# A token transform of Fourier channels folded by sums and differences, and a norm's weight moved into a rounding

## The chip, the cores and the metric

The kernel runs on one core of one Trainium2 chip. The metric is the device time in microseconds of one execution, the median over several runs. The engines are named TensorE (PE), VectorE (DVE), ScalarE (ACT), GpSimd (POOL) and SyncE (SP); they run their own queues in order and meet at semaphores.

## What is computed

Two layers of a hybrid transformer on 512 latent tokens and 256 context tokens, width 1024. After the input projection the columns feed three mixers: windowed attention (8 heads), bidirectional retention (4 heads of 64, with a group norm per head and direction) and a 2-D Fourier mixing of 256 channels in 4 groups. Then an output projection and a squared-ReLU MLP follow. The two parts that the change touches:

```python
def head_group_norm(o, g):
    mu = jnp.mean(o, axis=-1, keepdims=True)
    var = jnp.mean(jnp.square(o - mu), axis=-1, keepdims=True)
    y = (o - mu) * lax.rsqrt(var + EPS)
    return y.reshape(o.shape[0], o.shape[1], -1) * g.astype(jnp.float32)

def fourier_mix(u, w):
    b, l, _ = u.shape
    uf = u.astype(jnp.float32).reshape(b, l, FOURIER_GROUPS, FOURIER_DIM)
    y = jnp.fft.fft2(uf, axes=(1, 3), norm='ortho').real
    return jnp.einsum('blgc,gcd->blgd', y, w.astype(jnp.float32)).reshape(b, l, FOURIER_WIDTH).astype(u.dtype)

def ret_out(o_f, o_b, gf, gb):
    y = (head_group_norm(o_f, gn_g) * jax.nn.silu(gf.astype(jnp.float32))
         + head_group_norm(o_b, gn_g) * jax.nn.silu(gb.astype(jnp.float32)))
    return y.astype(gf.dtype)
```

The last layer computes latent tokens only (the context still gives keys and values).

## The kernel before

Tokens stand in tiles of 128: NL = 4 tiles of latent tokens, and NT = 6 with the context's two. The order of all work is written out by hand, engine by engine; nothing is scheduled. Large products (projections, MLP) are done as three products of rounded parts: a weight `W` and an activation `A` are each split in a high part in the rounded type fp32r and the rest (`Whi`, `Wlo`, `Ahi`, `Alo`). ScalarE rounds, GpSimd subtracts for the weights (L568, L572), VectorE or GpSimd for the activations. The mixers' own products are in fp32.

**The stage of the change** stands in each layer between the input projection and the retention. `Pu` holds the Fourier channels by token, `Pg` the two gates after their silu, `Pr` keys and values of the retention.

- TensorE: turns queries and keys (L1669), multiplies decayed keys with values (`key_values`, L1877, ten steps `e` of four matmuls in two groups: eight ahead of the transform, two within it), transforms the tokens of `Pu` by tables of cosines and sines (L1892: for each of four token tiles, two tables `s` and two halves `c` of the channels; 257 columns; sums in psA for the cosines and psB for the sines). In layer 0 the context follows (L1902, 129 columns, in psS) and, when ScalarE and VectorE have copied all of it out, the channel transform of the context (L1913). Then the retention starts in `psA` (L1936), `psS` (L1958, L1944).
- VectorE: centres the values (`centre`, L1381, L1382), then makes the running states `SD` out of the key-value products in PSUM (`states`, L1415: ten steps of four small instructions, each step after the one two before it), then copies the sine half out of psB, the second half mirrored with its sign turned (L1424, L1426). Then it serves the retention (L1456, L1442, L1467, L1468, L1472).
- ScalarE: rounds half of the keys (`key_hi`, L917) when the third token tile is done, copies psA out (L923, L924), in layer 0 the context (L929, L930), then the other half of the keys.
- GpSimd: decays the keys (L654, ten products of two SBUF tensors), the queries of the first two tiles (L662, four), multiplies the gates `Pg` with the group norm's weight `gng` (L670, one for each token tile, which VectorE's L1467 waits for by `gg_ready`), clears `klk` (L676) and subtracts the rounded keys (L683).
- SyncE: loads the tables, a token tile at a time, in two buffers of `modraw` and one of its own, `dft3`. The weight `gng` is loaded to all partitions by `tmp_load` (L407).

In the retention the normed, gated sum of both directions is turned by TensorE into channels by tokens (L1669) and rounded into `Ahi` (L964, ScalarE, both 128-channel halves in one instruction) and `Alo` (L1472, VectorE).

`rows` and `parT` hold the small parameters: rows of 128 loaded at the start (L414 to L419), turned once by TensorE, so that each becomes a column of `parT`.

## Time and profile before

| | us |
|---|---|
| median of three runs | 1614.09 |
| the runs | 1612.60, 1614.09, 1614.53 |
| the profiled execution | 1613.24 |
| its span in the profile | 1611.3 |

The profile is of one execution. The span runs from the first to the last instruction; 1.9 us of the execution's time lie around it. Start times are counted from the span's start. Lengths of single TensorE instructions overlap, since matmuls are pipelined: how long one holds the engine is read from start to start. The same holds, by some 0.1 us, for ScalarE and VectorE.

### The profile page before, as it was taken

Reading aid. Unit: us, or ns where it says so; the run is one execution under the profiler, and the core shown is the slowest. Engines: PE = TensorE matmul, PEld = TensorE weight load, DVE = VectorE, ACT = ScalarE, POOL = GpSimd, SP = SyncE. Lnnn points to the kernel's source line nnn. Section 1 sums busy time; section 2 is a strip of 40 time slices with the busy share of each in tenths; the row PEclk is TensorE's granted clock in tenths of the full one; section 3 lists DMA queues with packets and bytes.
Section 4 is the critical chain, followed back from the end, with each engine's and each line's share of the span. In section 5 each row is a group of like instructions: output and inputs, shape, how many; then the busy total and the mean of one; then the engine's idle time right before and its main releaser. Section 6 shows DMA issues by size and latency. Waiting matters only on the chain.

```text
span 1611.3 us, 22758 instructions
## 1 busy us (share of the span) xinstructions
PE 1566.2 (97%) x8730; PEld 1343.1 (83%) x8730; DVE 916.9 (57%) x1440; ACT 590.0 (37%) x958; POOL 651.2 (40%) x355
## 2 busy tenths in 40 slices
PE   6899999999999999999999999999999999999999
PEld 2688888988888888888888888888897788888887
DVE  5778977766765656445454668696644433333322
ACT  4532246752532221222212244434753522323222
POOL 1426678922333322232232453337004444444442
PEclk9899999999999999999999999999999999999999
DMA  9344203024233444354343533222002233333333
GB/s 330 98 131 129 75 27 109 26 66 131 85 105 118 131 122 131 89 156 131 110 128 103 153 98 103 66 88 71 17 1 79 78 93 93 103 91 101 94 97 100
DMA packets 170616, 163.43 MB, mean 101 GB/s; under 512 B 6672, under 2 KB 134176, under 8 KB 170528
## 3 DMA queue, kind: packets, MB, share of 16 engines
q1 hardware_dynamic: 170528, 162.20, 33.0%
q8 instruction: 63, 1.03, 0.3%
q14 instruction: 25, 0.20, 0.0%
HBM read 160.08 MB, written 2.10 MB: 101 GB/s over the span
## 4 chain that ended last, share of the span: by engine, by line
PE 90%; DVE 3%; issue 2%; ACT 2%; DMA 2%; POOL 1%; SPq 0%; POOLq 0%; ACTq 0%
PE psA L2043 10%; PE psB L2043 10%; PE psA L2044 10%; PE psA L2045 10%; PE psB L2044 10%; PE psB L2045 10%; PE ps L2018 4%; PE psS L1669 2%; PE psA L1827 2%; PE psA L1828 2%; PE psA L1829 2%; PE psB L1827 2%; PE psB L1828 2%; PE psB L1829 2%; PE ps L1669 1%
## 5 line engine op out<-in xcount | busy, mean ns | idle before, releaser
L568 POOL TENSOR_TENSOR Wlo<-raw,Whi 128x1024 fp32r<-128x1024 f32 x156 | 379.9, 2436 | 787.2 <-ACT Whi L734 787.2
L734 ACT ACTIVATE Whi<-raw 128x1024 fp32r<-128x1024 f32 x181 | 191.7, 1060 | 695.9 <-PE psB L2045 350.9
L2043 PE MATMUL psB<-Ahi,Whi 128*128 128x512 f32 (+1 forms) x432 | 154.5, 358 | 1.8 <-POOL Wlo L714 1.1
L2043 PE MATMUL psA<-Ahi,Whi 128*128 128x512 f32 (+1 forms) x424 | 152.1, 359 | 3.4 <-POOL Wlo L568 1.7
L2044 PE MATMUL psB<-Alo,Whi 128*128 128x512 f32 (+1 forms) x432 | 153.8, 356 | 0.0
L2045 PE MATMUL psB<-Ahi,Wlo 128*128 128x512 f32 (+1 forms) x432 | 153.7, 356 | 0.0
L2044 PE MATMUL psA<-Alo,Whi 128*128 128x512 f32 (+1 forms) x424 | 150.7, 355 | 0.0
L2045 PE MATMUL psA<-Ahi,Wlo 128*128 128x512 f32 (+1 forms) x424 | 150.7, 355 | 0.0
L1310 DVE SCALAR_TENSOR_TENSOR X<-psB,modT,X 128x256 f32<-128x256 f32 (+1 forms) x104 | 67.2, 665 | 130.5 <-PE psB L2045 130.4
L2043 PE MATMUL psA<-Hhi,Whi 128*128 128x512 f32 (+1 forms) x368 | 131.8, 358 | 3.1 <-DVE X L1310 2.9
L2043 PE MATMUL psB<-Hhi,Whi 128*128 128x512 f32 (+1 forms) x368 | 131.6, 358 | 0.1
L2044 PE MATMUL psB<-Hlo,Whi 128*128 128x512 f32 (+1 forms) x368 | 131.3, 357 | 0.0
L2045 PE MATMUL psB<-Hhi,Wlo 128*128 128x512 f32 (+1 forms) x368 | 131.1, 356 | 0.0
L2044 PE MATMUL psA<-Hlo,Whi 128*128 128x512 f32 (+1 forms) x368 | 130.8, 356 | 0.0
L2045 PE MATMUL psA<-Hhi,Wlo 128*128 128x512 f32 (+1 forms) x368 | 130.8, 355 | 0.0
L1310 DVE SCALAR_TENSOR_TENSOR X<-psA,modT,X 128x256 f32<-128x256 f32 (+1 forms) x104 | 67.0, 663 | 92.3 <-PE psA L2045 92.2
L1140 DVE SCALAR_TENSOR_TENSOR macc<-modraw,csil,macc 128x512 f32<-128x512 f32 x126 | 113.7, 959 | 9.8 <-DMA modraw<-in_w_mod_dram 9.8
L1535 DVE TENSOR_TENSOR Hlo<-Ab,Hhi 128x512 fp32r<-128x512 f32 (+2 forms) x68 | 72.7, 1070 | 54.5 <-ACT Hhi L1016 54.5
L1533 DVE TENSOR_TENSOR Ab<-psA,Tb 128x512 f32<-128x512 f32 (+2 forms) x34 | 26.7, 785 | 129.4 <-ACT Tb L1008 129.4
L2043 PEld LDWEIGHTS psA<-Ahi,Whi 128*128 128x128 f32 x424 | 80.1, 189 | 16.3 <-POOL Wlo L568 2.4
L2043 PEld LDWEIGHTS psB<-Ahi,Whi 128*128 128x128 f32 x432 | 81.7, 189 | 14.0 <-POOL Wlo L714 1.5
L2045 PEld LDWEIGHTS psB<-Ahi,Wlo 128*128 128x128 f32 x432 | 81.6, 189 | 11.7
(352 smaller groups left out, 3575.1 us busy)
## 6 DMA issues: line engine op xcount, KB each, us to landing
raw<-in_w_ff_dram SPq DMA_DIRECT2D x135, 512.0 KB, 4.1
modraw<-in_w_mod_dram SPq DMA_DIRECT2D x72, 512.0 KB, 4.3
raw<-in_w_in_dram SPq DMA_DIRECT2D x36, 512.0 KB, 3.8
modst<-in_w_mod_dram SPq DMA_DIRECT2D x16, 512.0 KB, 5.9
raw<-in_w_out_dram SPq DMA_DIRECT2D x16, 512.0 KB, 3.7
modat<-in_w_mod_dram SPq DMA_DIRECT2D x8, 512.0 KB, 4.2
macc<-in_w_ff_dram SPq DMA_DIRECT2D x5, 512.0 KB, 3.7
Xin<-in_x_dram SPq DMA_DIRECT2D x8, 256.0 KB, 8.1
```

The costliest lines, as they stand in the source:

```text
L568: nc.gpsimd.tensor_tensor(Wlo[:, s, :], raw[:, s, :], Whi[:, s, :], ALU.subtract).then_inc(S["lo_done"], 1)
L734: nc.scalar.activation(whis[slot], raws[slot], ACT.Copy).then_inc(S["hi_done"], 1)
L1140: ins = V.scalar_tensor_tensor(out=acc[:, s, :], in0=src[:, kk * MCH:(kk + 1) * MCH], scalar=col, in1=acc[:, s, :], op0=ALU.mult, op1=ALU.add)
L1310: last = V.scalar_tensor_tensor(out=X[:, m, c0:c1], in0=pair[p][:, c0:c1], scalar=modT[:, l, 8 * chunk + m, s:s + 1], in1=X[:, m, c0:c1], ...
L1535: V.tensor_tensor(Hlo[:, hpar, k, c0:c1], Ab[:, k % 2, c0:c1], Hhi[:, hpar, k, c0:c1], ALU.subtract).then_inc(S["h_lo"], 1)
L1827: mm(out, ah, wh, start=first, stop=False)
L1828: mm(out, ah, wl, start=False, stop=False)
L1829: last = mm(out, al, wh, start=False, stop=fin)
L2018: last = mm((ps6, ps7)[b % 2][:, h * HD:(h + 1) * HD], PTs[:, it % 2, i * P:(i + 1) * P], Pk[:, kt, P + (h // 4) * HD:P + (h // 4 + 1) * H ...
L2043: mm(dst[:, c0:c1], wh, hi_[:, i, c0:c1], start=first, stop=False)
L2044: mm(dst[:, c0:c1], wh, lo_[:, i, c0:c1], start=False, stop=False)
L2045: last = mm(dst[:, c0:c1], wl, hi_[:, i, c0:c1], start=False, stop=fin)
```

## The change

The transform of the tokens uses that a discrete Fourier transform over 512 tokens, split by four, needs only products over 128 tokens. With x0 to x3 the four token tiles of `Pu`, VectorE makes x0+x2, x1+x3, x0-x2, x1-x3, and from the first two their sum and difference (`folds`, six instructions of 128x256, all from SBUF to SBUF; in layer 0 two more for the context, x4+x5 and x4-x5). They stand in VectorE's queue between the centring and the states. TensorE multiplies the sum with a table for the frequencies 0, 4, 8, ..., the difference with one for 2, 6, 10, ..., and x0-x2 and x1-x3 with two for the odd ones. Each product holds a cosine part and a sine part, and writes every fourth or every second column of psA, half a bank for the channels' first half and half for the second. psB is no longer used for it. The context is split by two in the same manner. The table for a layer is one load of 128x768 (before: four of 128x514), for the context 128x256.

Since cosines and sines now stand in the same bank, ScalarE copies one half of the channels out and VectorE the other, in four instructions each instead of two. Two columns that are always zero are cleared by GpSimd.

The group norm's weight is no longer multiplied into the gates on GpSimd (L670 goes, and so does its broadcast load). It is loaded as four rows beside the other small parameters, turned with them, and applied as a scale for each partition where the turned result is rounded: L964 becomes two instructions of ScalarE, one for each half, and L1472 two of VectorE.

TensorE in layer 0, from the key-value products to the retention, before (`modraw` and `dft` are the tables, `ret_scratch` the decayed keys):

```order
L1877 MATMUL ps<-Pr,ret_scratch 128x128 x8
L1877 MATMUL psS<-Pr,ret_scratch 128x128 x8
L1892 MATMUL psA<-modraw,Pu 128x257 x2
L1892 MATMUL psB<-modraw,Pu 128x257 x2
L1892 MATMUL psA<-modraw,Pu 128x257 x2
L1892 MATMUL psB<-modraw,Pu 128x257 x2
L1892 MATMUL psA<-dft,Pu 128x257 x2
L1892 MATMUL psB<-dft,Pu 128x257 x2
L1877 MATMUL ps<-Pr,ret_scratch 128x128 x4
L1892 MATMUL psA<-modraw,Pu 128x257 x2
L1892 MATMUL psB<-modraw,Pu 128x257 x2
L1902 MATMUL psS<-modraw,Pu 128x129 x8
```

and after (here `ret_scratch` holds the folds as well):

```order
L1894 MATMUL ps<-Pr,ret_scratch 128x128 x8
L1894 MATMUL psS<-Pr,ret_scratch 128x128 x8
L1910 MATMUL psA<-modraw,ret_scratch 128x128 x4
L1894 MATMUL ps<-Pr,ret_scratch 128x128 x4
L1910 MATMUL psA<-modraw,ret_scratch 128x256 x4
L1919 MATMUL psS<-modraw,ret_scratch 128x128 x4
```

The last key-value step moved from behind three quarters of the transform to behind its first, short half.

VectorE in layer 0, from the last centring on, before:

```order
L1382 SCALAR_TENSOR_TENSOR Pr<-vm,Pr 128x256
L1415 SCALAR_TENSOR_TENSOR SD<-SD,CD,ps 64x64 x16
L1415 SCALAR_TENSOR_TENSOR SD<-SD,CD,psS 64x64 x16
L1415 SCALAR_TENSOR_TENSOR SD<-SD,CD,ps 64x64 x8
L1424 COPY ret_scratch<-psB 128x2x257
L1426 TENSOR_SCALAR ret_scratch<-psB 128x2x255
```

and after:

```order
L1378 SCALAR_TENSOR_TENSOR Pr<-vm,Pr 128x256
L1420 TENSOR_TENSOR ret_scratch<-Pu 128x256
L1421 TENSOR_TENSOR ret_scratch<-Pu 128x256
L1422 TENSOR_TENSOR ret_scratch<-Pu 128x256
L1423 TENSOR_TENSOR ret_scratch<-Pu 128x256
L1425 TENSOR_TENSOR ret_scratch<-ret_scratch 128x256
L1426 TENSOR_TENSOR ret_scratch<-ret_scratch 128x256
L1429 TENSOR_TENSOR ret_scratch<-Pu 128x256
L1430 TENSOR_TENSOR ret_scratch<-Pu 128x256
L1411 SCALAR_TENSOR_TENSOR SD<-SD,CD,ps 64x64 x16
```

Eight instructions now stand ahead of the states; in layer 1 it is six. The diff, cut to its core:

```diff
@@ SyncE
-            sp.dma_start(gng[:, :], a["ret_gn_g"][l].partition_broadcast(P)).then_inc(S["tmp_in"], 16)
+        sp.dma_start(rows[48:52, 1, :], a["ret_gn_g"].rearrange("l (t p) -> (l t) p", p=P)).then_inc(con, 16)
-            for k in range(2):
-                m_load(w + k, (w + k) % 2, dft_home(l, k)[:, 0:2 * FL], a["dft_lat"][k])
-            if l:
-                sp.wait_ge(S["mod_used"], DFT_FIRST[0] + 3 - MOD0)
-            sp.dma_start(dft3[:, :], a["dft_lat"][2]).then_inc(S["dft_in"], 16)
...
+            m_load(w, w % 2, dft_home(w, LAT_W), a["dft_lat"])
+            if l == 0:
+                m_load(w + 1, (w + 1) % 2, dft_home(w + 1, CTX_W), a["dft_ctx"])
@@ GpSimd
-            for t in range(TT[l]):
-                pool.wait_ge(S["p_ready"], evac_index[l, 3, t])
-                nc.gpsimd.tensor_tensor(Pg[:, t, :].rearrange("p (d n) -> p d n", d=2), Pg[:, t, :].rearrange("p (d n) -> p d n", d=2),
-                                        gng[:, :].unsqueeze(1).to_broadcast([P, 2, 256]), ALU.mult).then_inc(S["gg_ready"], 1)
+            nc.gpsimd.memset(zs_at(1)[:, :, 0:FL:FL - 1], 0.0).then_inc(S["zs_zero"], 1)
@@ ScalarE
-            za = psA[:, :].rearrange("p (a b) -> p a b", a=2)
-            nc.scalar.activation(zs_at(0)[:, :, 0:FL], za[:, :, 0:FL], ACT.Copy)
-            nc.scalar.activation(zs_at(0)[:, :, FL:LAT], za[:, :, LAT - FL:0:-1], ACT.Copy).then_inc(S["za_evac"], 1)
+            za = psA[:, 0:512]
+            nc.scalar.activation(zs_at(0)[:, 0, 0:FL], za[:, 0:FL], ACT.Copy)
+            nc.scalar.activation(zs_at(0)[:, 0, FL:LAT], za[:, LAT - FL:0:-1], ACT.Copy)
+            nc.scalar.activation(zs_at(1)[:, 0, 1:FL - 1], za[:, FL:LAT], ACT.Copy)
+            nc.scalar.activation(zs_at(1)[:, 0, FL:LAT], za[:, LAT - 1:FL - 1:-1], ACT.Copy, scale=-1.0).then_inc(S["za_evac"], 1)
...
+                    for q in range(2):
+                        last = nc.scalar.activation(Ahi[:, 4 + q, t * P:(t + 1) * P], (ps6, ps7)[t % 2][:, q * P:(q + 1) * P], ACT.Copy, scale=parT[:, 48 + 2 * l + q:49 + 2 * l + q])
@@ VectorE
+            def folds():
+
+                dve.wait_ge(S["unit_done"], UP * (l + 1))
+                dve.wait_ge(S["p_ready"], evac_index[l, 4, NL - 1])
+                x = [Pu[:, t, :] for t in range(NT)]
+                V.tensor_tensor(fold_half(0), x[0], x[2], ALU.add).then_inc(S["fold_half"], 1)
+                V.tensor_tensor(fold_half(1), x[1], x[3], ALU.add).then_inc(S["fold_half"], 1)
+                V.tensor_tensor(fold(2), x[0], x[2], ALU.subtract).then_inc(S["fold_ready"], 1)
+                V.tensor_tensor(fold(3), x[1], x[3], ALU.subtract).then_inc(S["fold_ready"], 1)
+                dve.wait_ge(S["fold_half"], 2 * l + 2)
+                V.tensor_tensor(fold(0), fold_half(0), fold_half(1), ALU.add).then_inc(S["fold_ready"], 1)
+                V.tensor_tensor(fold(1), fold_half(0), fold_half(1), ALU.subtract).then_inc(S["fold_ready"], 1)
+                if l == 0:
+                    dve.wait_ge(S["p_ready"], evac_index[0, 4, NT - 1])
+                    V.tensor_tensor(fold(4), x[4], x[5], ALU.add).then_inc(S["fold_ready"], 1)
+                    V.tensor_tensor(fold(5), x[4], x[5], ALU.subtract).then_inc(S["fold_ready"], 1)
+
+            folds()
             dve.wait_ge(S["sd_zero"], 1)
             dve.wait_ge(S["prep_act"], 15 * (l + 1))
             states(0, NST_E)
@@ TensorE
+            pe.wait_ge(S["fold_ready"], (0, 6)[l] + 4)
+            lat_tab = dft_home(w, LAT_W)
+            for k, (first, step, t0, n) in enumerate(((0, 4, 0, P), (2, 4, P, P), (1, 2, 2 * P, 2 * P), (1, 2, 4 * P, 2 * P))):
+                if k == 2:
                     key_values(8, NST_E)
...
+                for c in range(2):
+                    last = mm(psA[:, c * 512 + first:c * 512 + 512:step], fold(k)[:, c * P:(c + 1) * P], lat_tab[:, t0:t0 + n], start=(k < 3), stop=(k != 2))
```

## Rows read from the trace of the kernel before

**Rows 1.** The page's first part: busy time of TensorE over the whole span

```profile
PE 1566.2 (97%) x8730; PEld 1343.1 (83%) x8730; DVE 916.9 (57%) x1440; ACT 590.0 (37%) x958; POOL 651.2 (40%) x355
```

**Rows 2.** Timeline, TensorE, layer 0: start us, length, line, tiles, count [idle, releaser]

```profile
214.88 1.03 PE L1892 MATMUL psA<-modraw,Pu 128*128 128x257 f32 x4
...
220.09 1.05 PE L1877 MATMUL ps<-Pr,ret_scratch 128*128 128x128 f32 x8
...
222.72 1.95 PE L1902 MATMUL psS<-modraw,Pu 128*128 128x129 f32 x16
...
226.06 1.97 PE L1913 MATMUL psB<-Zc,WCS 128*128 128x256 f32 x8 [1.39 <-ACT Zc L930]
```

**Rows 3.** Timeline, VectorE, layer 0

```profile
209.86 0.43 DVE L1382 SCALAR_TENSOR_TENSOR Pr<-vm,Pr 128x256 f32<-128x256 f32 x1
210.20 0.41 DVE L1381 TENSOR_REDUCE vm<-Pr 128x4 f32<-128x256 f32 x1
210.65 0.43 DVE L1382 SCALAR_TENSOR_TENSOR Pr<-vm,Pr 128x256 f32<-128x256 f32 x1
212.51 4.05 DVE L1415 SCALAR_TENSOR_TENSOR SD<-SD,CD,ps 64x64 f32<-64x64 f32 x16 [1.44 <-PE ps L1877]
...
221.25 2.01 DVE L1415 SCALAR_TENSOR_TENSOR SD<-SD,CD,ps 64x64 f32<-64x64 f32 x8 [0.61 <-PE ps L1877]
...
223.30 0.69 DVE L1424 COPY ret_scratch<-psB 128x514 f32<-128x514 f32 x1
```

**Rows 4.** Timeline, GpSimd, layer 0: three L654 singly, then the four L662

```profile
209.93 0.83 POOL L654 TENSOR_TENSOR ret_scratch<-Pr,ZE 128x256 f32<-128x256 f32 x1
...
210.72 0.83 POOL L654 TENSOR_TENSOR ret_scratch<-Pr,ZE 128x256 f32<-128x256 f32 x1
...
211.51 0.61 POOL L654 TENSOR_TENSOR ret_scratch<-Pr,ZE 128x256 f32<-128x256 f32 x1
...
214.94 2.78 POOL L662 TENSOR_TENSOR ret_scratch<-rqT,XQ 128x256 f32<-128x256 f32 x4
```

**Rows 5.** Timeline, VectorE, layer 0, earlier: instructions queued beside GpSimd's

```profile
146.15 4.91 DVE L1140 SCALAR_TENSOR_TENSOR macc<-modraw,csil,macc 128x512 f32<-128x512 f32 x3
```

**Rows 6.** Timelines, TensorE and then VectorE, layer 1

```profile
1108.74 1.03 PE L1892 MATMUL psB<-modraw,Pu 128*128 128x257 f32 x4
...
1111.57 0.72 PE L1936 MATMUL psA<-rqT,rkT 64*128 64x128 f32 x8 [1.80 <-ACT ret_scratch L924]
...
1121.17 2.00 PE L1944 MATMUL psS<-Pr,ret_scratch 128*128 128x64 f32 x16
...
1123.30 1.16 PE L1958 MATMUL psS<-SD,ret_scratch 128*128 128x128 f32 x8
...
1099.14 4.05 DVE L1415 SCALAR_TENSOR_TENSOR SD<-SD,CD,ps 64x64 f32<-64x64 f32 x16 [11.10 <-PE ps L1877]
...
1108.14 2.01 DVE L1415 SCALAR_TENSOR_TENSOR SD<-SD,CD,ps 64x64 f32<-64x64 f32 x8 [0.87 <-PE ps L1877]
...
1113.64 2.08 DVE L1442 TENSOR_TENSOR qs<-qT,qs 64x512 fp32r<-64x512 f32 x1
```

**Rows 7.** Four stretches: length, PE busy (count), the others; PEclk, DMA share, GB/s

```profile
942.80:946.20 3.40, 3.40 (x28) 3.28 (x27) 1.48 (x2) 0.63 (x1) 0.18 (x1) 1.00 0.50 154
...
949.90:953.30 3.40, 3.40 (x19) 3.40 (x18) 0.48 (x1) 1.70 (x3) 2.98 (x2) 0.50 0.00 0
...
965.90:968.70 2.80, 0.00 (x0) 0.00 (x0) 2.80 (x4) 0.77 (x2) 1.78 (x1) 1.00 0.68 187
...
45.50:55.60 10.10, 7.52 (x20) 5.54 (x21) 9.72 (x17) 5.74 (x12) 1.81 (x1) 0.50 0.20 60
```

**Rows 8.** Timeline, SyncE's queue, start of the kernel

```profile
2.99 0.28 SPq L419 DMA_DIRECT2D rows<-in_c_ctx_dram  x1
```

**Rows 9.** Groups by form, ScalarE: busy, mean ns of one | idle before

```profile
L811 ACT ACTIVATE decay<-tmpt,lgt 128x128 f32<-128x128 f32 x16 | 5.1, 389 | 0.0
...
L964 ACT ACTIVATE Ahi<-ps 128x256 fp32r<-128x256 f32 x10 | 3.7, 373 | 0.6 <-PE ps L1669 0.6
```

More of the change, by code:

```diff
@@ L24 @@
 FL, FC = LAT // 2 + 1, CTX // 2 + 1
+LAT_W, CTX_W = 6 * P, 2 * P
 GROUPS = [(0, 512), (512, 512), (1024, 512), (1536, 512), (2048, 256)]
@@ L256, in mod_loads, with dft_home, fold, fold_half @@
     def mod_loads(w):
-        return (w - MOD0) // 2 + 1 - ((4 if w % 2 else 5) if w >= LATE else 0)
-    def dft_home(l, k):
-        return dft3[:, :] if k == 2 else modraw[:, (DFT_FIRST[l] + k % 3) % 2, :]
-    def dft_wait(engine, l, k):
-        w = DFT_FIRST[l] + k % 3
-        if k == 2:
-            engine.wait_ge(S["dft_in"], 16 * (l + 1))
-        else:
-            engine.wait_ge(mod_in[w % 2], 16 * (mod_loads(w) + k // 3))
+        return (w - MOD0) // 2 + 1 - ((5 if w % 2 else 6) if w >= LATE else 0)
+    def dft_home(w, n):
+        return modraw[:, w % 2, 0:n]
+    def fold(i):
+        return rs[:, 18 + i // 2, (i % 2) * 256:(i % 2) * 256 + 256]
+    def fold_half(i):
+        return rs[:, 6 + i, 0:256]
     def thirds(x):
@@ L1471, in retention @@
                     dve.wait_ge(S["rT_hi"], r + 1)
-                    V.tensor_tensor(Alo[:, 4:6, t * P:(t + 1) * P], (ps6, ps7)[t % 2][:, 0:256].rearrange("p (a b) -> p a b", a=2),
-                                    Ahi[:, 4:6, t * P:(t + 1) * P], ALU.subtract).then_inc(S["rT_lo"], 1)
+                    for q in range(2):
+                        last = V.scalar_tensor_tensor(out=Alo[:, 4 + q, t * P:(t + 1) * P], in0=(ps6, ps7)[t % 2][:, q * P:(q + 1) * P], scalar=parT[:, 48 + 2 * l + q:49 + 2 * l + q],
+                                                      in1=Ahi[:, 4 + q, t * P:(t + 1) * P], op0=ALU.mult, op1=ALU.subtract)
+                    last.then_inc(S["rT_lo"], 1)
                 if 1 <= s < TT[l] + 1:
@@ L2285, in dft @@
         return (np.stack([np.cos(w), np.sin(w)]) / np.sqrt(n * HD)).astype(f)
-    lat = dft(LAT).reshape(2, NL, P, FL).transpose(1, 2, 0, 3).reshape(NL, P, 2 * FL)
-    ctx = dft(CTX).reshape(2, 2, P, FC).transpose(2, 0, 1, 3).reshape(P, 4 * FC)
+    (lc, ls), (xc, xs) = [[part[0:P] for part in dft(n)] for n in (LAT, CTX)]
+    odd = np.arange(1, LAT // 2, 2)
+    turn = np.where(odd % 4 == 1, f(1), f(-1))
+    lat = np.concatenate([lc[:, 0::4], ls[:, 4:FL - 1:4], lc[:, 2::4], ls[:, 2::4], lc[:, odd], ls[:, odd],
+                          -turn * ls[:, odd], turn * lc[:, odd]], 1).astype(f)
+    ctx = np.concatenate([xc[:, 0::2], xs[:, 2:FC - 1:2], xc[:, 1::2], xs[:, 1::2]], 1).astype(f)
     return {"table": tab, "dft_lat": np.ascontiguousarray(lat), "dft_ctx": np.ascontiguousarray(ctx)}
```

74 lines of the change are left out of this document (34 added, 40 removed).

## The prediction

> **What bounds the kernel now.** I read the page first: TensorE is busy for 97% of the span [rows 1], so a microsecond counts where TensorE waits, or where its own work shrinks while nothing else is late. The change touches one place in each of the two layers, so I then read the order of time there, engine by engine. In layer 0 TensorE runs the token transform from 214.88 (L1892), one step of the key-value products in its middle (L1877 at 220.09), then the context's transform (L1902 at 222.72), and stops until 226.06 [rows 2]. The reader should see the other queue beside it: VectorE turns the key-value products into states (L1415) from 212.51, eight of the forty from 221.25, and only then copies psB out, from 223.30 [rows 3]. TensorE's row at 226.06 names ScalarE's last copy of the context (L930) as what it waited 1.39 us for [rows 2]. So at the end of this stage two chains arrive close together: VectorE's (states, two copies of 0.6) at about 224.6 and ScalarE's at 225.9. In layer 1, with no context, it is TensorE's last products at 1108.74, VectorE's last states at 1108.14 and the two copies after them, TensorE again at 1111.57 [rows 6]; that row names ScalarE's copy, but by its length VectorE's second copy ended last, 0.1 us before. TensorE's matmuls here are therefore not alone on the path: the forty states take as long as they do.
>
> **Matmuls removed.** A 128x257 product is two instructions; four take 0.87 us (214.88, 1.03 is the end of the last), so 0.43 a product; a 128x128 one 0.22 (eight instructions to 220.98, where 0.89 have passed) [rows 2]. Sixteen of 257 columns (6.9 us) become four of 128 and four of 256 (0.9 + 1.7 = 2.6): 4.3 us less in each layer; eight context products of 129 columns (1.8) become four of 128 (0.9). The new products write every second or fourth column of psA. No row shows that; if it cost double it would still be inside the waits found below, so it is zero on the path and at worst 1 us.
>
> **Layer 0, the queue of VectorE.** The eight sums and differences (`folds`) stand between the centring and the states. Centring ends at 211.05 (last step 210.65 + 0.43; the next instruction can start 0.34 after such a one, as at 209.86 and 210.20) and the first state starts at 212.51 [rows 3]: 1.46 us are free. At their own pace, 0.34 each, the folds need 2.7 and push the states by 1.3. But GpSimd runs ten products of two SBUF operands (L654) until 214.94 and four more (L662) after it [rows 4], and each fold too reads two tensors from SBUF. What that does the rows show. Beside the centring steps one L654 takes 0.83 us, alone 0.61, and beside VectorE they start 0.785 apart [rows 4]: GpSimd loses about 0.2 each time, less than one centring step. When VectorE has such instructions queued without a gap it is VectorE that is slow: three L1140 of 512 elements, beside a long and a short GpSimd product, take 4.91 us, 1.6 each [rows 5]. So the two take turns, one instruction each. Folds back to back against L654 then go at 0.785 each: the first reads after the product that started at 210.72, and ends at 211.85; the sixth at 215.8, the eighth, against L662, at 217.4. The states start at 217.4 instead of 212.51.
>
> From there the sum runs on: TensorE may start the transform at 215.9 (it needs the sixth fold), does the two short pairs until 216.8, and waits for the first eight states until 219.5 before L1877's last step (0.9) and the long pairs (1.7): 222.1. The context waits for 32 states, 217.4 + 8.2 = 225.6, ends at 226.6, and ScalarE's four copies of it end at 227.7. The forty states, now without the 0.6 us in which VectorE waited for TensorE, end at 217.4 + 10.24 = 227.7. The copy out is now four instructions of 255 or 257 columns at 0.34 = 1.4, for two that took 1.2 [rows 3]. TensorE goes on at 229.1, after 226.06: **+3.1**. What is late next is VectorE; the shorter matmuls lie wholly in its shadow. The lower bound for this term is folds at their own pace: states at 213.8, copies done at 225.5, TensorE at 225.7: -0.4.
>
> The Trainium skill ("SBUF — State Buffer", section "Who interferes with whom") says that a VectorE instruction with two SBUF inputs contends with a GpSimd one that reads SBUF, and that the later one blocks for the whole of the other's. By it a fold waits for a full product, and eight cost 8 x (0.34 + 0.61) = 7.6 us instead of 6.3: TensorE 1.3 us later still. The trace agrees with the rule in kind (0.83 us against 0.61 [rows 4]), not in size, and its own 0.785 is what I use.
>
> **Layer 1.** VectorE sits idle for 11 us before the states, until 1099.14 [rows 6], and all of Pu was copied out before TensorE began the turns, some 6 us earlier, so the six folds are hidden whichever pace they have; if that cover were gone they would cost 2 to 4.7 us. TensorE ends its transform at 1105.4 instead of 1109.7. VectorE's states lose the 0.87 us that they waited for L1877 [rows 6] and end at 1109.3; four copies, 1.4; TensorE starts at 1110.8 instead of 1111.57: -0.8. The gain norm product L670 is gone from GpSimd, so the subtraction of the keys (L683) runs before 1111 and no longer beside VectorE's L1442, which took 2.08 us in a first go of two. TensorE, otherwise without a pause from 1111.57, was late by 0.2 at 1121.17 and by 0.3 at 1123.30, where sixteen L1944 need 1.8 [rows 6]: -0.5 more, at least 0. **-1.25** for the layer.
>
> **Rounding with the weight.** One L964 of 256 columns, 0.37 us, becomes two of 128 with a scale from a tensor; such an instruction (L811) takes 0.39 [rows 9] and can start some 0.3 after the one before it. In the last two steps this stands between TensorE's turn and the softmax's table load, 0.3 each: +0.45 a layer, **+0.9**; between 0 (if hidden) and 1.5. On VectorE one instruction becomes two, 0.1 us each time, hidden by the turn to the next step. Dropping L670 from GpSimd is worth nothing beyond the above: L1467 was never late for it.
>
> **The start.** One more DMA (four rows) stands in SyncE's queue ahead of the first weights. The one before it takes 0.28 us and starts at 2.99 [rows 8], and what follows is the stream of loads that the start of the kernel waits for. **+0.35**, at least 0 and at most 0.5. The two broadcasts of the weight (L407) and three table loads a layer less are off the path: their destinations are long filled.
>
> **The clock.** TensorE would stand still in layer 0 from 216.8 to 219.5, 222.1 to 225.6 and 226.6 to 229.1, in layer 1 from 1105.4 to 1110.8. In this trace an idle stretch of 2.8 us (965.9) left the granted clock at 1.00, 2.4 GHz; but it was 0.50, 1.2 GHz, in 45.5 to 55.6, after a stretch with 2.8 us of no work and gaps inside, and for 3.4 us at 949.9, after TensorE had summed squares with matmuls of one column for 2.6 us [rows 7]. 3.5 and 5.4 us are longer than what it held through. So I expect one fall in each layer. At 1.2 GHz 19 instructions start in 3.4 us for 28 [rows 7], 1.1 us lost; over 4 to 5 us, as after 51, 1.5 us. Take 1.45 twice: **+2.9**, between 0 and about 6.
>
> **Sum.** 3.1 - 1.25 + 0.9 + 0.35 + 2.9 = 6.0. The profiled execution took 1613.24 (span 1611.3): 1619.2. That is 0.85 below the median of the runs, 1614.09, so against the median the sum would be 1620; I keep the sum as it is, since one execution lies as well at one end of the runs as at the other.
>
> **Rivals.**
> A, forecast: turns at the port and a fall of the clock in each layer: 1619.2, own range 1616.8 to 1621.5. Chance 0.45.
> B: the turns, but the clock holds: 1616.3. For it: it held through 2.8 us. Chance 0.18, within 0.2% of 1614.09 (3.2 us).
> C, the other side (not slower): VectorE gets its eight folds in at 0.34 while GpSimd waits, as the centring steps did, which were not slowed themselves (0.43) [rows 3]; the whole rests on whether VectorE's queue without gaps keeps the port. It decides from the point at which the folds end before 214. Then layer 0 gives -0.4, the sum -0.4 - 1.25 + 0.9 + 0.35 = -0.4, 1612.8, and with one or two falls of the clock up to 1615.7. Against it: the 1.6 us of [rows 5]. Chance 0.18.
> D, faster: the transform's matmuls are the path after all, as they would be if the states' chain kept step with them; 4.3 + 0.9 in layer 0 and 4.3 in layer 1 are saved but for the folds' 1.3: some 8 us less, 1605. Against it: VectorE's chain ends at 224.6, 1.3 us ahead of TensorE's restart, whatever TensorE does. Chance 0.07.
> E: the clock stays at 1.2 GHz through much of the retention stage, whose matmuls are short (64 and 128 columns); each 3.4 us more costs 1.1 to 1.7. 1623 to 1628. Chance 0.12.
>
> A measurement of this kernel can tell about 0.2%, 3.2 us, from no change. Slower by more than that: most of A (0.4), E and the top of B, 0.57; within: 0.34; faster: D and a little of C, 0.09. The range leaves out D and the upper part of E: 1612.5 to 1623.5; A and B and C lie in it.
>
> **What would show it.** The time from the last centring step to the first state in layer 0: 6.3 us (A, B) or 2.7 (C); one fold at 0.75 to 0.8 us or at 0.42. GpSimd's ten L654 in 7.7 us. TensorE's restart: 229.5 in layer 0 with the start's 0.35, and, in layer 1, 1110.8 plus what came before. The granted clock below 1.00 in both places. The rounding's two activations at 0.39. I am wrong if TensorE restarts in layer 0 before 226, if the strided products themselves take several times 0.43, or if the stretch after retention is slower for another reason than these.

## The result, and the profile after

| | before | changed |
| --- | --- | --- |
| median of five runs each, us | 1613.62 | 1619.91 |
| ratio to before, 95% interval | | 1.0044, 1.0033 to 1.0055 |
| the profiled execution, us | 1613.24 | 1619.91 |
| its span, us | 1611.3 | 1617.9 |
| mean granted clock of TensorE | 0.996 | 0.991 |

The kernel became slower: by 6.3 us from median to median, and by 0.44%, which is 7.1 us, by the ratio, an estimate over all executions that need not be the quotient of the medians (1.0039). Run once more beside the experiments its ratio was 1.0054 (1.0035 to 1.0073). Medians and ratios here are of fast executions alone; beside them one of the changed kernel took 2232.67 us, at a mean granted clock of 0.65, and one of before 3156.01. The forecast was 1619.2.

The timelines of layer 0, VectorE first: start, length, engine, line, tiles, and in brackets the idle time before and what ended it. They answer to [rows 3].

```profile
210.47 0.43 DVE L1378 SCALAR_TENSOR_TENSOR Pr<-vm,Pr 128x256 f32<-128x256 f32 x1
210.81 0.83 DVE L1420 TENSOR_TENSOR ret_scratch<-Pu 128x256 f32<-128x256 f32 x1
211.57 0.83 DVE L1421 TENSOR_TENSOR ret_scratch<-Pu 128x256 f32<-128x256 f32 x1
...
216.09 0.94 DVE L1430 TENSOR_TENSOR ret_scratch<-Pu 128x256 f32<-128x256 f32 x1
216.96 4.04 DVE L1411 SCALAR_TENSOR_TENSOR SD<-SD,CD,ps 64x64 f32<-64x64 f32 x16
...
225.11 2.01 DVE L1411 SCALAR_TENSOR_TENSOR SD<-SD,CD,ps 64x64 f32<-64x64 f32 x8
227.15 0.43 DVE L1438 COPY ret_scratch<-psA 128x257 f32<-128x257 f32 x1
...
228.15 0.41 DVE L1441 TENSOR_SCALAR ret_scratch<-psA 128x255 f32<-128x255 f32 x1
```

Each fold takes 0.83 and starts 0.755 after the one before. The states begin at 216.96 instead of 212.51, and behind them stand the four copies: there is no idle time left in VectorE's queue. GpSimd beside it [rows 4]:

```profile
208.21 7.67 POOL L647 TENSOR_TENSOR ret_scratch<-Pr,ZE 128x256 f32<-128x256 f32 x10
```

And TensorE [rows 2]:

```profile
215.56 1.13 PE L1910 MATMUL psA<-modraw,ret_scratch 128*128 128x128 f32 x8 [0.41 <-DVE ret_scratch L1426]
219.10 2.05 PE L1894 MATMUL ps<-Pr,ret_scratch 128*128 128x128 f32 x8 [2.41 <-DVE SD L1411]
220.94 2.61 PE L1910 MATMUL psA<-modraw,ret_scratch 128*128 128x256 f32 x8
225.22 1.13 PE L1919 MATMUL psS<-modraw,ret_scratch 128*128 128x128 f32 x8 [1.67 <-DVE SD L1411]
228.67 3.22 PE L1930 MATMUL psB<-Zc,WCS 128*128 128x256 f32 x8 [2.31 <-DVE ret_scratch L1441]
231.82 1.09 PE L1953 MATMUL psA<-rqT,rkT 64*128 64x128 f32 x8
```

All four waits of TensorE are now ended by VectorE. It restarts at 228.67 (the first product after the last wait of the stage), before at 226.06. Layer 1, VectorE and then TensorE [rows 6]:

```profile
1100.11 2.59 DVE L1423 TENSOR_TENSOR ret_scratch<-Pu 128x256 f32<-128x256 f32 x1
...
1104.90 4.05 DVE L1411 SCALAR_TENSOR_TENSOR SD<-SD,CD,ps 64x64 f32<-64x64 f32 x16 [0.69 <-PE ps L1894]
...
1116.11 0.41 DVE L1441 TENSOR_SCALAR ret_scratch<-psA 128x255 f32<-128x255 f32 x1
```

```profile
1109.93 1.89 PE L1910 MATMUL psA<-modraw,ret_scratch 128*128 128x256 f32 x8
1116.63 1.21 PE L1953 MATMUL psA<-rqT,rkT 64*128 64x128 f32 x8 [4.81 <-DVE ret_scratch L1441]
1117.77 2.07 PE L1975 MATMUL psS<-SD,ret_scratch 128*128 128x128 f32 x8
```

The transform is out of TensorE's way by 1111.8, and TensorE waits 4.81 us for the states and the copies. That the new products write every second column of psA costs nothing that shows: eight instructions of 128x256 take 1.89 (1109.93), where L1913, of the same size, took 1.97 [rows 2].

Last, the stretches in which the granted clock was 0.50, which is 1.2 GHz (from:to, length, TensorE busy and its instructions, clock, DMA share, GB/s); they answer to [rows 7]. Between 25 us and the last two of the span, the trace of before has two such stretches: 10.2 us from 45.4, and 3.4 us from 949.9.

```profile
44.90:55.14 10.24, 7.19 (x20) 0.50 0.20 61
218.98:222.39 3.41, 3.29 (x12) 0.50 0.01 2
229.22:232.63 3.41, 3.41 (x15) 0.50 0.03 5
403.30:406.71 3.41, 3.41 (x18) 0.50 0.76 251
973.33:976.74 3.41, 3.41 (x18) 0.50 0.45 148
1116.69:1120.10 3.41, 3.41 (x18) 0.50 0.00 0
```

One more, of 3.4 us, is at 952.9, where before had its own at 949.9. The fall at 973.33 comes 0.3 us behind a wait of TensorE that the kernel before has too, the 2.8 us from 965.9 of [rows 7], after which the clock held:

```profile
973.05 0.36 PE L2060 MATMUL psA<-Hhi,Whi 128*128 128x256 f32 x1 [2.87 <-DVE X L1306]
```

**Where the 6.6 us of the span came in.** The same TensorE instruction was looked up in both traces, and the start of before taken from the start of after:

| TensorE's instruction | late by, us | step |
| --- | --- | --- |
| first turn after the projection, 204.79 | -0.30 | -0.30 |
| restart in layer 0, 228.67 | 2.61 | +2.91 |
| first L1961 of retention, 234.57 (fall at 229.2) | 3.93 | +1.32 |
| after the rounding's last tile, 271.36 | 4.02 | +0.09 |
| 437 (fall at 403.3) | 5.55 | +1.53 |
| 464.25, after a wait in the feed-forward | 4.57 | -0.98 |
| 923 to 973 (one fall in each trace) | 4.29 | -0.28 |
| 978 to 1099 (fall at 973.3) | 5.76 | +1.47 |
| restart in layer 1, 1116.63 | 5.06 | -0.70 |
| 1119.77 (fall at 1116.7) | 6.47 | +1.41 |
| 1129.43 | 6.13 | -0.34 |
| 1138.33, after the rounding's last tile | 6.51 | +0.38 |

### The profile page after: what moved, and what is told of

Same layout as the page of the kernel before. It is cut to its first block, busy times and chain, and to the rows that moved or that the text cites. A ratio compares the mean times of both kernels' runs of the same rounds, so it can differ in the third digit from the quotient of the medians.

```text
span 1617.9 us, 22707 instructions
## 1 busy us (share of the span) xinstructions
PE 1566.8 (97%) x8690; PEld 1341.9 (83%) x8690; DVE 924.0 (57%) x1468; ACT 592.7 (37%) x972; POOL 642.7 (40%) x349
## 4 chain that ended last, share of the span: by engine, by line
PE 91%; DVE 3%; ACT 2%; DMA 2%; issue 1%; POOL 1%; SPq 0%; ACTq 0%; DVEq 0%; POOLq 0%
PE psA L2060 10%; PE psB L2060 10%; PE psB L2061 10%; PE psA L2061 10%; PE psA L2062 10%; PE psB L2062 10%; PE ps L2035 4%; PE psS L1686 2%; PE psA L1844 2%; PE psA L1845 2%; PE psA L1846 2%; PE psB L1844 2%; PE psB L1846 2%; PE psB L1845 2%; PE ps L1686 1%; PE psS L1846 1%
## 5 line engine op out<-in xcount | busy, mean ns | idle before, releaser
L561 POOL TENSOR_TENSOR Wlo<-raw,Whi 128x1024 fp32r<-128x1024 f32 x156 | 381.8, 2448 | 784.0 <-ACT Whi L725 784.0
```

Of the source, the lines that this page charges most:

```text
L561: nc.gpsimd.tensor_tensor(Wlo[:, s, :], raw[:, s, :], Whi[:, s, :], ALU.subtract).then_inc(S["lo_done"], 1)
```

## Experiments

In each, the executions of the kernel before on the same chip are the measure (medians 1614.9, 1613.86, 1613.8 and 1614.42 in four groups). Behind a time stand, in brackets, its ratio to them and the ratio's 95% interval. "Net" of a shift means: after what TensorE was already late by at the first turn, or ahead of the stage, is taken off.

### The two halves of the change, each alone

`fold_alone` is the changed kernel with group norm's weight back on GpSimd; `weight_alone` is the kernel before with the weight in the rounding. The second one's core:

```
-  nc.scalar.activation(Ahi[:, 4:6, t * P:(t + 1) * P], (ps6, ps7)[t % 2][:, 0:256].rearrange("p (a b) -> p a b", a=2), ACT.Copy).then_inc(S["rT_hi"], 1)
+  for q in range(2):
+      last = nc.scalar.activation(Ahi[:, 4 + q, t * P:(t + 1) * P], (ps6, ps7)[t % 2][:, q * P:(q + 1) * P], ACT.Copy, scale=parT[:, 48 + 2 * l + q:49 + 2 * l + q])
+  last.then_inc(S["rT_hi"], 1)
```

> The changed kernel with group norm's weight put back where it was (product L670 on GpSimd, one rounding instruction per tile, broadcasts of the weight, no extra DMA at the start); the transform stays split by four. Theory: the 6.3 us of the change are the transform's: VectorE's queue in layer 0 (+2.9 at the restart), the granted clock after the waits (+1.3 to +1.5 a layer), -0.7 in layer 1, and the rounding adds 0.8 to 1.0. Then this kernel is 5.0 to 5.5 us slower than before, 1618.6 to 1619.1. Rival: the rounding and its weight are the larger part, since in both layers the stretch after the restart is the one that grows (3.9 to 4.4 in layer 0, 6.1 to 6.5 in layer 1): then it is 2 to 4 us above before, 1615.5 to 1617.5.

> The kernel before with the weight moved into the rounding alone (no L670, two activations and two VectorE instructions per tile, one more DMA at the start, three loads less); transform as before. Theory: +0.4 to +0.5 a layer at the last tile, where two activations stand between the turn and the softmax's table load, less 0.3 at the start: +0.5 to +0.9, 1614.1 to 1614.5. Layer 1's L1442 at 0.7 instead of 2.1 us and its restart otherwise as before. Rival: the weight is what costs, +2.5 to +4 (1616 to 1617.5).

Measured: `fold_alone` 1621.54 (ratio 1.0048, 1.0030 to 1.0066), `weight_alone` 1614.98 (1.0003, 0.9994 to 1.0011). The whole loss belongs to the transform; the weight costs nothing that can be told. `fold_alone` is 6.6 us above its group's before by the medians and 7.7 by the ratio (4.8 to 10.7), more than the 5.0 to 5.5 expected; one of its six executions took 1629.34. That the longer stretch after the restart was the rounding's, the rival, is out. On ScalarE the expected thing does happen. The last tile in layer 1, of before and then of `weight_alone`:

```profile
1129.29 0.39 ACT L964 ACTIVATE Ahi<-ps 128x256 fp32r<-128x256 f32 x1 [0.32 <-PE ps L1669]
1129.69 1.28 ACT L981 ACT_TABLE_LOAD   x1
```

```profile
1129.96 0.63 ACT L957 ACTIVATE Ahi<-ps,parT 128x128 fp32r<-128x128 f32 x2 [0.26 <-PE ps L1665]
1130.61 1.28 ACT L975 ACT_TABLE_LOAD   x1
```

From the turn's end to the table load 0.65 instead of 0.40. TensorE is later by 0.43 at 256 us, but 0.41 of it is given back at 268 us, where it waits for the softmax of a later item anyway; in layer 1 it is -0.48 by 1123.8 (GpSimd is free of L670) and +0.38 by 1132.7. VectorE's L1442 of before took 1.48 here, not the 0.7 expected: GpSimd's second subtraction of keys waits for ScalarE's rounding of them, starts at 1113.78 and still stands beside it.

### Folds later in the queue

`late4`, from the changed kernel, layer 0 only:

```
-  folds()
...
-  states(0, NST_E)
+  states(0, 4)
+  folds()
+  states(4, NST_E)
```

> The changed kernel; in layer 0 VectorE does the first 16 of the 40 states before its eight sums and differences, so that GpSimd's products have mostly ended when they come. Theory (turns at the port): the states start at 212.2 and the folds at 216.3, two of them at 0.78 and six at 0.34, 3.6 us instead of 6.3; the states end at 226.0, TensorE restarts at 227.5 instead of 228.67: 1.0 to 1.3 us less, 1618.7, and GpSimd's ten products end by 214.9. Rival: it is not GpSimd that makes the folds 0.755 apart but the folds themselves (a first pass over these tiles, a fixed cost in layer 0): they stay at 0.75, 6.0 us, and the restart stays at 228.4 to 228.7, 1619.9.

Measured: 1618.39 (1.0031, 1.0016 to 1.0046). VectorE in layer 0:

```profile
217.85 0.71 DVE L1420 TENSOR_TENSOR ret_scratch<-Pu 128x256 f32<-128x256 f32 x1
218.48 0.94 DVE L1421 TENSOR_TENSOR ret_scratch<-Pu 128x256 f32<-128x256 f32 x1
219.34 0.41 DVE L1422 TENSOR_TENSOR ret_scratch<-Pu 128x256 f32<-128x256 f32 x1
219.68 0.41 DVE L1423 TENSOR_TENSOR ret_scratch<-Pu 128x256 f32<-128x256 f32 x1
```

The first two, beside GpSimd's L655, take 0.71 and 0.94; from 219.1 on GpSimd only zeroes, and the other six go at 0.34. Eight folds in 3.6 us instead of 6.2, as the theory said; that the folds are slow by themselves is out. TensorE's restart gains less than the 1.0 to 1.3 expected, 0.65 net of the start's shift, since the transform now begins only at 220.91 and ScalarE's copies of the context come last there.

### What a turn is made of

`half_folds` lets the folds of layer 0 work on 128 of 256 columns (first line added, `c` being those columns; the transform takes the same 128 for both halves of the channels, so the second half's transform is left out and the result is not the kernel's), `stt_folds` writes them in the form of the centring steps (second line added):

```
-  V.tensor_tensor(fold(2), x[0], x[2], ALU.subtract).then_inc(S["fold_ready"], 1)
+  V.tensor_tensor(fold(2)[:, c], x[0], x[2], ALU.subtract).then_inc(S["fold_ready"], 1)
...
+  V.scalar_tensor_tensor(out=fold(2), in0=x[0], scalar=1.0, in1=x[2], op0=ALU.mult, op1=ALU.subtract).then_inc(S["fold_ready"], 1)
```

> The changed kernel; in layer 0 the eight sums and differences take 128 of their 256 columns, and the transform takes the same 128 for both halves (so the second half's transform is left out). Is the 0.755 us between folds the sum of both engines' work (0.34 and about 0.4), or one GpSimd product with VectorE's inside it? Theory (turns, where the wait for GpSimd's product sets the pace): a fold loses 0.14 us of its own work, the spacing falls to 0.6 to 0.66. Rival (a fold is taken up only at GpSimd's next boundary, and GpSimd's product of 0.61 plus a fixed cost is the period): the spacing stays at 0.74 to 0.76.

> The changed kernel with the sums and differences written as SCALAR_TENSOR_TENSOR (operand times 1.0, then plus or minus the other) as the centring steps are. Theory: the turns come from two tensors read from SBUF, whatever the form: 0.75 apart, as before, 1619.9. Rival: the form TENSOR_TENSOR alone takes turns, since centring's L1378 beside L647 takes 0.43: then the folds go at 0.34 to 0.45, the states start 2.5 to 3 us earlier, 1617.

Each ran once, for its trace (1617.56 and 1620.12 us). Measured, `half_folds` and then `stt_folds`:

```profile
212.03 0.70 DVE L1423 TENSOR_TENSOR ret_scratch<-Pu 128x128 f32<-128x128 f32 x1
212.65 0.70 DVE L1424 TENSOR_TENSOR ret_scratch<-Pu 128x128 f32<-128x128 f32 x1
```

```profile
211.91 0.83 DVE L1421 SCALAR_TENSOR_TENSOR ret_scratch<-Pu 128x256 f32<-128x256 f32 x1
212.67 0.83 DVE L1422 SCALAR_TENSOR_TENSOR ret_scratch<-Pu 128x256 f32<-128x256 f32 x1
```

Half the columns shorten the period, from the start of one fold to the next, from 0.755 to 0.62, by 0.135. That is the difference between undisturbed instructions of VectorE with two tensors from SBUF (0.41 with 256 columns in `late4`, 0.29 with 128, L1359 at 203.70 in the changed kernel), so the fold's own work counts in full. The rest, 0.755 less the 0.336 between undisturbed folds, is 0.42. The simplest reading is that it is the part of GpSimd's product during which a fold can't read; a product takes 0.61 alone [rows 4], and undisturbed ones start 0.57 apart (ten L654 in 5.76, 1096.56 in before). The form makes no difference. Why the centring steps of the same form were spared beside GpSimd's short products is not shown; in them every second instruction, the reduction, reads one tensor only. Beside a long product they were not spared: one L1382 took 2.29 at 206.42 in before, with L568 of 2.37 started at 206.06. The Trainium skill ("SBUF — State Buffer", "Who interferes with whom") says that a VectorE instruction with two SBUF inputs contends with a GpSimd one that reads SBUF, and these runs agree. The section calls the ports that the two share an exclusive lock. If that held for the whole of each instruction, a period would be a fold and a whole product, 0.34 and 0.57 to 0.61, so 0.91 to 0.95; 0.755 is what was measured.

### The clock

`clock_held` gives TensorE something to do in the waits of the change: matmuls whose result nobody reads, called idle matmuls from here on. The calls of `hold` stand in layer 0 before L1894's last step (two matmuls), before the context (one) and before the restart (two), in layer 1 before the restart (five):

```
+  def hold(bank, n):
+      for i in range(n):
+          mm(bank, fold(0)[:, 0:P], lat_tab[:, 0:512], start=True, stop=True)
...
+  hold(psB[:, 0:512], (2, 5)[l])
   pe.wait_ge(S["za_evac"], l + 1)
```

> The changed kernel with matmuls of 512 columns into psB, whose result nobody reads, in TensorE's waits: two and one and two in layer 0 (before L1894's last step, before the context, before the restart), five in layer 1 before the restart. Theory: 2.5 to 4 us of the change's 6.3 are the granted clock, which falls to 1.2 GHz at 219.0, 229.2 and 1116.7: with TensorE kept at work it stays at 1.00 there, TensorE is 1.3 less late by 255 us and 1.4 less in layer 1: 2.7 less, 1617.2, and the executions lie closer together than those of the changed kernel. Rival: the matmuls stand in the way of the restart themselves, or the clock falls all the same: 1619.5 to 1621.

Measured: 1618.15 (1.0022, 1.0013 to 1.0030), where the changed kernel has 1.0044 and 1.0054: 3.5 us less by the first, with some 2 either way. By the medians it is 4.3 above before instead of 6.3, 2.0 less. Stretches of its trace:

```profile
226.27:229.68 3.41, 3.41 (x11) 0.51 0.00 0
1112.00:1117.00 5.00, 4.50 (x11) 1.00 0.01 2
1117.00:1120.40 3.40, 3.40 (x33) 1.00 0.03 5
```

In layer 1 the clock stays at 2.4 GHz, and 33 instructions start in 3.4 us after the restart, where the changed kernel had 18. In layer 0 one fall of two is left; at 1.2 GHz the last two idle matmuls took 2.8 us and pushed the restart by 0.7. In the two traces, net of the start, the held kernel gains 0.7 behind layer 0's restart and 1.6 in layer 1. So the clock in these waits is a third to half of the loss, and the runs don't tell more exactly.

### Where the copies stand

`scalar_copies`: ScalarE copies psA's upper half, four instructions of which one is shown; VectorE ends with the states.

```
-  V.tensor_copy(zs_at(0)[:, 1, 0:FL], zb[:, 0:FL])
+  nc.scalar.activation(zs_at(0)[:, 1, 0:FL], zb[:, 0:FL], ACT.Copy)
```

> The changed kernel with the second half of the transform (psA's upper 512 columns) copied out by ScalarE instead of VectorE, four more activations in its queue. Theory: VectorE's chain (folds, states, copies) sets the restart in both layers, so taking the 1.4 us of copies from its end brings the restart to 227.7 in layer 0 (ScalarE's copies of the context are then last) and to 1115.3 plus the shift of layer 0 in layer 1: 1.0 and 1.3 less, in all 1.5 to 2.3 us less, 1617.6 to 1618.4. Rival: ScalarE's queue is as late as VectorE's, and its four more copies of 0.3 put the context's copies behind: restart 228.6 in layer 0, only layer 1's 1.2 gained, 1618.7 to 1619.

Measured: 1627.34 (1.0071, 1.0052 to 1.0089), 1618.6 to 1629.3. The waits behave as the theory said: net of the shift before them, the restart in layer 0 is 0.9 sooner than in the changed kernel (228.39, ScalarE last), in layer 1 it is 1.5 sooner. And yet the kernel is slower, for this:

```profile
1109.60:1112.90 3.30, 0.04 (x1) 1.00 0.00 0
1114.54:1135.02 20.48, 20.48 (x103) 0.50 0.24 68
```

The clock, after a wait of 3.3 us, fell and stayed at 1.2 GHz for 20.5 us of retention, all of it in TensorE's way: TensorE is 1.4 late at the restart and 10.6 late by 1139 us. That is rival E of the prediction. A wait of 3.3 instead of 4.8 us did not save the clock. Nor does the wait alone decide: one execution of the six took 1618.6, at a mean granted clock of 0.990 where the others have 0.982 to 0.986. The changed kernel has such an execution too, one in ten: 1629.25 in `changed_again`, at 0.984, where its other nine lie from 1619.6 to 1622.9 at 0.987 to 0.992. `fold_alone` and `late4` have one each (1629.34, 1628.74, both 0.984).

### Do the falls at 403 and 973 belong to the change?

`delayed_before2` is the kernel before with 4.35 us of idle matmuls ahead of layer 0's L1913:

```
+  for i in range(5):
+      mm(psB[:, 0:512], WCS[:, 0, 0, :], zs_at(0)[:, 0], start=True, stop=True)
```

> The kernel before with nothing of the change, but five matmuls of 512 columns (into psB, read by nobody) after layer 0's waits and ahead of the context's second transform: TensorE at work for 4.35 us more, everything after it later by that, and no idle stretch added. What it asks: do the falls of the clock that the changed kernel shows at 403 and 973, after one-column matmuls that the kernel before has too, come with a later start of the stage alone? Theory (they have nothing to do with the change's waits; which of the stages falls is a matter of when it comes): such falls appear here too, and the time is 4.35 to 6.5 us above before, the excess over 4.35 being up to 2.2. Rival (they are the consequence of the change's idle stretches or of its falls at 219 and 229): the clock stays at 1.00 at about 400 and falls only at about 950 as in before, and the time is 4.2 to 4.6 above before.

Measured: 1619.23 (1.0029, 1.0020 to 1.0039), 4.7 above before.

```profile
403.43:406.84 3.41, 3.41 (x19) 0.51 0.69 236
950.70:954.10 3.40, 3.40 (x33) 1.00 0.17 56
973.43:976.84 3.41, 3.25 (x15) 0.50 0.49 154
```

Both falls are there without anything of the change, and the one that before has at 949.9 is not. What TensorE does ahead of the three places is the same in every kernel: one-column matmuls that sum squares ahead of the first two, a wait of 2.9 us ahead of the third. That the falls come with a later start fits, but is not the whole of it. At about 400 the clock falls with TensorE 4.45 late there (`stt_folds`) and not with 4.56 or 4.59 (`late4`, `half_folds`); it falls in `gpsimd_folds_held2`, where TensorE is less than 0.4 us from its place in before. What decides is not shown. Over ten executions the extra falls are worth about 0.4 us beyond the 4.35 that were put in (by the ratio, from -1.1 to +1.9), less than the 2.2 that this one profile shows (TensorE 4.02 later than before at 230, 6.25 at 977), and their mean granted clock, 0.993 to 0.995, is that of before's (0.993 to 0.996). So in the difference of two profiles such a fall is luck; in the medians little of it is left.

### A version without the queue

`gpsimd_folds_held`, `gpsimd_folds` and `gpsimd_folds_held2` take the folds of layer 0 off VectorE, and the copies too, as in `scalar_copies`. The latent folds (`G` is GpSimd's tensor_tensor) stand between its last two weight splits, with the half sums `m` in macc and the results in parts of modraw that the tables leave free; the context's two stand behind the decayed queries. In `gpsimd_folds_held2` TensorE has two idle matmuls before it waits for the context's folds, one before layer 0's restart, three before layer 1's.

```
+  low_part(18)
+  G(m[0], x[0], x[2], ALU.add).then_inc(S["fold_half"], 1)
+  G(m[1], x[1], x[3], ALU.add).then_inc(S["fold_half"], 1)
+  G(fold0(2), x[0], x[2], ALU.subtract).then_inc(S["fold_ready"], 1)
...
+  low_part(19)
...
   decayed_queries(1)
+  nc.gpsimd.tensor_tensor(fold(4), Pu[:, 4, :], Pu[:, 5, :], ALU.add).then_inc(S["fold_ctx"], 1)
```

> A version meant to keep what the change saves. From the changed kernel: group norm's weight back as before; in layer 0 the six latent sums and differences run on GpSimd at 201 to 205 us, before its last weight split (L561), into free parts of modraw, with halves in macc, and the context's two on GpSimd after the first decayed queries; VectorE goes from centring to the states; ScalarE copies psA's upper half too; matmuls that nobody reads hold the clock in the waits (three and one in layer 0, five in layer 1). Theory: states in layer 0 at 212.3, ended at 222.6, TensorE restarts at 223 instead of 226.06 of the kernel before (-2.9), and in layer 1 1.9 sooner (states' end sets it, no copies behind them): -4.8 in all, 1609 to 1610. Rival: GpSimd's six products take turns with VectorE's L1359 and L1363 at 200 to 204, which TensorE's turns wait for, and what is won in the stages goes there: within 2 us of before, 1612 to 1615.

Measured: 1617.61 (1.0018, 1.0009 to 1.0026), a miss. In this version the weight was back on GpSimd, and the zeroing that TensorE's restart waits for stood behind it:

```profile
222.17 7.38 POOL L687 TENSOR_TENSOR Pg<-Pg,gng 128x512 f32<-128x512 f32 x6
229.49 0.11 POOL L689 MEMSET ret_scratch<- 128x4 f32 x1
229.53 0.11 POOL L691 MEMSET Zc<- 128x4 f32 x1
```

TensorE restarted at 229.85; the states had ended at 225.25 and ScalarE's copies at 227.3. With the weight in the rounding, as the change has it, those products are gone:

> From the changed kernel, with its rounding (group norm's weight stays in it): in layer 0 the six latent sums and differences on GpSimd at 203 us, the context's two on GpSimd behind the decayed queries, GpSimd's zeroing right behind them; ScalarE copies psA's upper half as well. Nothing holds the clock. Theory: in the version with the weight restored, TensorE's restart of layer 0 at 229.85 waited for GpSimd's zeroing at 229.5, behind six products L687 of 7.4 us; without them the zeroing is at 222.5 and the states' end sets the restart: 225.5 with a start late by 1.3, so 1.8 sooner than before; 1.9 sooner in layer 1; rounding +0.9. Before the clock that is -2.8; the clock falls in one or both layers, +1.3 to +9 (as in the version with ScalarE's copies, where it lasted 20 us): 1612.5 to 1620, and executions that lie far apart. Rival: the restart stays later than 227, for another wait: above 1616 even with the clock held.

> The same with matmuls that nobody reads in TensorE's waits, fewer than in the first version and each ended before the work that follows: two before the wait for the context's sums, one before layer 0's restart, three before layer 1's. Theory: -2.8 as above and the clock held in layer 1 and mostly in layer 0: 1611 to 1613, 1 to 3 us below before. Rival: the falls of the clock in layer 0 come whatever is put there (with such matmuls it fell at 226.3 once), +1.3, and the rounding's stage is longer than its two instructions: 1613.5 to 1615.5.

> The changed kernel once more, on the chip and beside the runs of before that the two versions below share. Theory: its time is one sum with a part that varies, the falls of the clock, of which the trace has three more than before's in 218 to 230 and 1117 and two single ones at 403 and 973: 1618 to 1622, ratio 1.003 to 1.0055. Rival (the first result was one chip's): within 0.2% of before.

Measured on one chip: `changed_again` 1620.62 (1.0054, 1.0035 to 1.0073); `gpsimd_folds` 1624.24 (1.0052, 1.0035 to 1.0069), its twelve executions in two groups, four from 1614.6 to 1615.6 and eight from 1623.8 to 1627.5; `gpsimd_folds_held2` **1612.67 (0.9988, 0.9979 to 0.9997)**, all executions from 1610.2 to 1614.7 (before on that chip: 1611.4 to 1617.3). TensorE of the last:

```profile
223.03 1.13 PE L1950 MATMUL psS<-modraw,ret_scratch 128*128 128x128 f32 x8 [0.51 <-DVE SD L1441]
...
225.55 1.97 PE L1962 MATMUL psB<-Zc,WCS 128*128 128x256 f32 x8 [0.53 <-ACT Zc L954]
...
1112.10 0.72 PE L1985 MATMUL psA<-rqT,rkT 64*128 64x128 f32 x8 [0.75 <-issue]
```

The restart comes 0.9 before that of the kernel before in layer 0 (net of a start late by 0.35) and 2.2 before it in layer 1, and the clock is 1.00 behind both. In layer 0 half of what was expected is missing: GpSimd's six folds (202.67 to 208.17) stand beside VectorE's work ahead of the centring, where two products of 128 columns take 0.70 and 0.71 instead of 0.29. The centring begins at 206.70 instead of 204.39, and TensorE waits for it:

```profile
213.48 2.02 PE L1915 MATMUL ps<-Pr,ret_scratch 128*128 128x128 f32 x16 [1.66 <-DVE Pr L1408]
```

The same kernel without the six idle matmuls lies 11 to 15 us above that version's median in eight of twelve executions. That this is the clock, the granted clock of each execution shows: 0.989 to 0.990 in the four short ones, 0.981 to 0.985 in the eight long ones. By the group means that is some 19 us more at 1.2 GHz (an estimate: twice the difference, times the span), and the groups lie some 10 us apart; in `scalar_copies` 20.5 us cost 9.2. That it is again layer 1 is not shown, since the profile of `gpsimd_folds` is of a short execution (1615.5). There TensorE waited as long ahead of layer 1's retention as in `scalar_copies`, and the clock stayed at 1.00 behind it:

```profile
1113.60 0.72 PE L1974 MATMUL psA<-rqT,rkT 64*128 64x128 f32 x8 [3.32 <-ACT ret_scratch L947]
```

The gain of `gpsimd_folds_held2` is small, 0.03 to 0.21% by its interval. No run gave the kernel before the same copies on ScalarE and the same idle matmuls, so how much of the gain is the split's own is not shown.

## Why the prediction was right, point by point

**Layer 0's queue** (+3.1): right, +2.91. The folds took turns with GpSimd, 0.755 each against 0.785 taken from [rows 4], the states began at 216.96 against 217.4, TensorE restarted at 228.67 against 229.1 (0.3 of it is the earlier start). `late4`, `half_folds` and `stt_folds` show that the turns with GpSimd, and not the folds by themselves, make the 6.2 us; rival C, in which the folds keep their own pace, is out. The matmuls removed were worth nothing on the path, as reckoned.

**Layer 1** (-1.25): right in kind, -0.70 at the restart and -0.34 by 1129: -1.04. The folds were not free of GpSimd there either, a single one took 2.59 beside a whole weight split (L1423, 1100.11; GpSimd's L561 1099.99 to 1102.41). The cover was not the 11 us of idle time in [rows 6] but the 5.8 from the last copy of Pu (1099.10) to the states (1104.90), the "some 6 us" of the prediction; the folds left 0.69 of it. Behind the restart L1442's successor took 0.69 instead of 2.08, as forecast, but not because the subtraction of the keys had run long before: its second half stood from 1115.81 to 1117.62, past the restart, and VectorE came to the step only at 1119.19.

**Rounding** (+0.9): this term was mis-sized. `weight_alone` gives 0.5 us by its ratio, with an interval from -1.0 to +1.8, and the table of the changed kernel 0.09 in layer 0 and 0.38 in layer 1. The two activations cost 0.25 ahead of the table load and TensorE 0.4 a layer, as reckoned; the step that failed is that this goes on to the end: in layer 0 a later wait of TensorE takes it back.

**Start** (+0.35): failed. The added DMA stands at 3.31 in SyncE's queue and takes 0.30, and still TensorE is 0.30 earlier at 204.79. Across the traces of this study the same instruction lies -0.35 to +1.27 from before's: `delayed_before2`, which is the kernel before up to there, at -0.35, `fold_alone` without the DMA at +1.23 and `gpsimd_folds_held2` with it at +0.35. The start varies from one execution to the next by more than the term.

```profile
2.99 0.27 SPq L417 DMA_DIRECT2D rows<-in_c_ctx_dram  x1
3.31 0.30 SPq L418 DMA_DIRECT2D rows<-in_ret_gn_g_dram  x1
3.64 1.42 SPq L426 DMA_DIRECT2D modst<-in_w_mod_dram  x3
```

**Clock** (+2.9): right in sum, +1.32 and +1.41 behind the two restarts, and `clock_held` gives it from the other side (3.5 by the ratios, some 2 either way; 2.0 by the medians). In layer 0 it fell twice. Through the first fall, at 219.0, TensorE was at work for 3.29 of the 3.41 us, but it waited 1.67 for VectorE right behind it, and so it cost nothing at the restart. The stretch of 2.8 us through which [rows 7] saw the clock hold was no rule: here it fell at the end of a wait of 2.41 (219.0), just behind one of 2.31 (229.2), and at 973.33 behind that very stretch, while in `gpsimd_folds` it held behind one of 3.32.

**Not in the sum**: what came in between 271 and 978, with the falls at 403 and 973: +1.53 - 0.98 - 0.28 + 1.47, together 1.7. It makes up what start and rounding had too much, so the forecast is nearer to the measured time than its steps were, and that is luck: without it the steps of the table add up to 4.8, where the forecast had 6.0. `delayed_before2` shows that such falls come without the change.

**Rivals.** B (the clock holds) is what `clock_held` nearly is, 4.3 above before by the medians where B has 3.1. D (the matmuls are the path) is out: 4.3 us less of them in each layer, and TensorE waits 2.31 and 4.81 for others. E did not come in the profile of the changed kernel, but one of its ten executions fits it, 1629.25 at a mean clock of 0.984, a little above E's 1623 to 1628. In the profile of `scalar_copies` it came: the clock stayed low for 20.5 us and TensorE lost 9.2 us, 1.5 for each 3.4, inside the 1.1 to 1.7 that E was reckoned with.

## What to carry to other kernels

Shorter matmuls bring nothing where another engine's queue ends the stage; work that is put ahead of that queue costs its length, and more where both VectorE and GpSimd read two tensors from SBUF. The kernel with the split was faster than before, by 0.12% (0.03 to 0.21), only when its sums were taken off the queue, the copies behind the states were given to ScalarE, and TensorE was kept at work in the waits; the copies alone, the held clock alone, and sums and copies without the held clock all stayed slower than before, and so did all three with the weight's products back on GpSimd. Where a stage is made emptier for TensorE, count the clock with it, and compare many executions rather than two profiles.
